# A hybrid decoder layer on one core: a third Strassen block in ten gate/up pairs, and the fold moved

## The reference

```python
def swiglu(h, w_gate, w_up, w_down):
    return (jax.nn.silu(h @ w_gate) * (h @ w_up)) @ w_down
...
        h = rmsnorm(x, norm_ffn_g[l])
        x = x + swiglu(h, w_ffn_gate[l], w_ffn_up[l], w_ffn_down[l])
    return rmsnorm(x, norm_final_g)
```

## Time and profile before

| | |
|---|---|
| median of 3 runs | 1755.81 us (1754.05 to 1756.22) |
| the profiled execution's own time | 1754.56 us |
| its span, first to last instruction | 1752.2 us |
| busy share: TensorE matmul, weight load, VectorE, ScalarE | 99%, 82%, 73%, 56% |
| granted TensorE clock, mean | 0.999 of full speed (2.4 GHz) |

### The profile page before, as it was taken

The page is one execution under the profiler, slowest core; times in us unless marked ns, Lnnn a source line. Parts: engine busy times, 40 slices in busy tenths (PEclk is TensorE's granted clock), DMA queues, the critical chain, the costliest instruction groups (busy, mean ns, idle before and its releaser), DMA issues.

```text
span 1752.2 us, 20308 instructions
## 1 busy us (share of the span) xinstructions
PE 1740.3 (99%) x7926; PEld 1444.7 (82%) x7926; DVE 1283.2 (73%) x1399; ACT 972.8 (56%) x1209; POOL 28.4 (2%) x54
## 2 busy tenths in 40 slices
PE   9999999999999999999999999999999999999998
PEld 7888888888888888888888888888888888888886
DVE  7577677887575757655565578888888788888787
ACT  6767678554555555544455465555545545555554
POOL 1000000000000000000000000000000000000000
PEclk9999999999999999999999999999999999999999
DMA  8565665666565655556755455566666565666664
GB/s 284 173 200 167 204 193 162 199 204 204 163 209 168 216 168 189 172 186 209 249 184 189 138 177 181 192 194 194 196 209 207 184 209 192 192 192 194 215 202 158
DMA packets 176047, 338.22 MB, mean 193 GB/s; under 512 B 10704, under 2 KB 15312, under 8 KB 175696
## 3 DMA queue, kind: packets, MB, share of 16 engines
q1 hardware_dynamic: 173232, 327.72, 59.3%
q0 software_dynamic: 1296, 5.24, 0.9%
q10 hardware_dynamic: 1424, 3.97, 0.6%
HBM read 334.80 MB, written 2.10 MB: 192 GB/s over the span
## 4 chain that ended last, share of the span: by engine, by line
PE 97%; DVE 1%; ACT 0%; DMA 0%; issue 0%; ACTq 0%; DVEq 0%; POOLq 0%; POOL 0%
PE group L468 29%; PE group L470 29%; PE group L469 29%; PE side L468 2%; PE side L469 2%; PE side L470 2%; PE side L531 2%; DVE w_lo L1199 0%; DMA x_T_in<-in_x_T 0%; PE side L649 0%; PE side L633 0%; PE side L587 0%; PE side L586 0%; PE side L585 0%; DVE x_res L1551 0%
## 5 line engine op out<-in xcount | busy, mean ns | idle before, releaser
L817 ACT ACTIVATE w_hi<-w_raw 128x1024 fp32r<-128x1024 f32 x612 | 622.9, 1029 | 543.5 <-PE group L470 447.9
L1199 DVE TENSOR_TENSOR w_lo<-w_raw,w_hi 128x1024 fp32r<-128x1024 f32 x612 | 712.6, 1186 | 286.3 <-ACT w_hi L817 280.3
L468 PE MATMUL group<-w_hi,x_hi 128*128 128x512 f32 x1466 | 575.6, 393 | 0.5 <-DVE w_lo L1274 0.3
L470 PE MATMUL group<-w_hi,x_lo 128*128 128x512 f32 x1466 | 571.0, 390 | 0.0
L469 PE MATMUL group<-w_lo,x_hi 128*128 128x512 f32 x1466 | 570.5, 389 | 0.0
L468 PEld LDWEIGHTS group<-w_hi,x_hi 128*128 128x128 f32 x1466 | 275.3, 188 | 58.9 <-DVE w_lo L1199 2.0
L470 PEld LDWEIGHTS group<-w_hi,x_lo 128*128 128x128 f32 x1466 | 275.1, 188 | 57.9
L469 PEld LDWEIGHTS group<-w_lo,x_hi 128*128 128x128 f32 x1466 | 275.4, 188 | 55.6
L817 ACT ACTIVATE w_hi<-w_sums 128x1024 fp32r<-128x1024 f32 x84 | 89.1, 1061 | 148.1 <-PE group L470 107.2
L1199 DVE TENSOR_TENSOR w_lo<-w_sums,w_hi 128x1024 fp32r<-128x1024 f32 x84 | 102.5, 1223 | 56.5 <-ACT w_hi L817 56.4
L468 PE MATMUL group<-w_hi,v_hi 128*128 128x512 f32 x296 | 115.9, 392 | 0.0
(11 more groups left out here) (304 smaller groups left out, 1707.4 us busy)
## 6 DMA issues: line engine op xcount, KB each, us to landing
w_raw<-in_w_in SPq DMA_DIRECT2D x223, 512.0 KB, 4.2
w_raw<-in_w_ffn_gate SPq DMA_DIRECT2D x88, 512.0 KB, 4.0
w_raw<-in_w_ffn_up SPq DMA_DIRECT2D x88, 512.0 KB, 4.6
w_raw<-in_w_ffn_down SPq DMA_DIRECT2D x88, 512.0 KB, 4.8
w_raw<-in_w_rnn_proj SPq DMA_DIRECT2D x32, 512.0 KB, 4.6
w_raw<-in_w_attn_proj SPq DMA_DIRECT2D x32, 512.0 KB, 4.3
w_raw<-in_w_mix_out SPq DMA_DIRECT2D x32, 512.0 KB, 4.6
w_raw<-in_w_xkv SPq DMA_DIRECT2D x16, 512.0 KB, 3.8
```

What stands on the lines that cost most here:

```text
L468: nc.tensor.matmul(out, h, whi[:, s, k, :], start=start, stop=False)
L470: return nc.tensor.matmul(out, l, whi[:, s, k, :], start=False, stop=stop)
L817: nc.scalar.activation(whi[:, s, ks], src[:, ks], ACT.Copy).then_inc(hi_ready[s], 1)
L1199: V_.tensor_tensor(wlo[:, s, ks], src[:, ks], whi[:, s, ks].bitcast(F32), ALU.subtract).then_inc(w_ready[s], 1)
```

## The change

The plan of the ten up pairs goes from two blocks to three: "O0 O1 W3 O2 O4 W5 O6 O7" becomes "O0 O2 W1 O4 W3 O6 W5 O7", 22 chunks instead of 20. The first up pair keeps a plan of its own with one block (W3). The sums of the left factor, made in that first pair, cover three blocks instead of two (k-pairs 1, 3, 5), in buffers of their own. In all pairs with blocks, ScalarE copies P1 in iteration last_sum-1 instead of last_sum+1. In the ten up pairs alone, where the last D stands third from the end, VectorE makes the first two additions of the fold in iteration last_sum and the other two in last_sum+1, one iteration sooner each than by the rule that holds elsewhere.

```diff
--- before.py
+++ after.py
@@ -62,7 +62,7 @@
 GROUPS += [("cross_out", _j, NB) for _j in range(KG)]
 
 
-UP_PLAN = "O0 O1 W3 O2 O4 W5 O6 O7".split()
+UP_PLAN = "O0 O2 W1 O4 W3 O6 W5 O7".split()
 RNN_PLANS = {0: "T0+1 O3 W2 O5 W4 O6 O7".split(), 2: "O0 O1 W2 O3 O5 W4 O6 O7".split()}
 KEY_PLAN = "O0 O1 W3 O2 O4 W5 O6 O7".split()
 FIRST_UP_PLAN = "O0 O1 O2 O4 W3 O5 O6 O7".split()
@@ -216,14 +216,18 @@
         chi = at("cross_hi", S + 8 * K1, [NB, SEQ], F32R)
         clo = at("cross_lo", S + 12 * K1, [NB, SEQ], F32R)
         fold = at("fold", S, [2, TT, GW])
-        both = at("x2_both", S + 4 * K1, [2, CK, SEQ])
-        x_sum = at("x2_sums", S, [2, 4, P])
-        xs_hi = at("x2_sums_hi", S + 12 * K1, [2, 4, P], F32R)
+        both = at("acts_both", S + 4 * K1, [2, CK, SEQ])
+        x_sum = at("acts_sums", S, [2, 4, P])
+        xs_hi = at("rnn_sums_hi", S + 12 * K1, [2, 4, P], F32R)
+        us_hi = at("x2_sums_hi", S + 8 * K1, [3, 4, P], F32R)
+        us = at("x2_sums", U + 24 * K1, [3, 4, P])
+        x2_both = at("x2_both", S, [3, CK, SEQ])
         fs_hi, fs_lo = at("inner_sums_hi", U + 24 * K1, [4, 4, P], F32R), at("inner_sums_lo", V + 24 * K1, [4, 4, P], F32R)
 
         STAGE = [region(4 * K1), region(4 * K1)]
         ks_hi = at("x_sums_hi", STAGE[0], [2, 4, P], F32R)
-        xs_lo = at("x2_sums_lo", STAGE[1], [2, 4, P], F32R)
+        us_lo = [at("x2_sums_lo0", STAGE[1], [2, 4, P], F32R), at("x2_sums_lo1", S + 14 * K1, [1, 4, P], F32R)]
+        xs_lo = at("acts_sums_lo", STAGE[1], [2, 4, P], F32R)
         stage = [at(f"stage{n}", STAGE[n], [TT, GW]) for n in range(2)]
         silu = stage[0]
 
@@ -515,13 +519,13 @@
                         products(P1, xh[:, k0, tok0], xl[:, k0, tok0], s, 0, begin, end)
                         last = products(gps[p0][:, 0, :], xh[:, k1, tok0], xl[:, k1, tok0], s, 1, False, False)
                     if kind == "B":
-                        last = products(gps[p1][:, 0, :], sh[:, w, 3, :], sl[:, w, 3, :], s, 1, False, False)
+                        last = products(gps[p1][:, 0, :], sh[:, w, 3, :], sl[w][:, 3, :], s, 1, False, False)
                     if kind == "C":
-                        products(Q5, sh[:, w, 0, :], sl[:, w, 0, :], s, 0, begin, end)
+                        products(Q5, sh[:, w, 0, :], sl[w][:, 0, :], s, 0, begin, end)
                         last = products(gps[p0][:, 1, :], xh[:, k1, tok1], xl[:, k1, tok1], s, 1, False, False)
                     if kind == "D":
-                        products(P7, sh[:, w, 2, :], sl[:, w, 2, :], s, 0, begin, end)
-                        last = products(P6, sh[:, w, 1, :], sl[:, w, 1, :], s, 1, begin, end)
+                        products(P7, sh[:, w, 2, :], sl[w][:, 2, :], s, 0, begin, end)
+                        last = products(P6, sh[:, w, 1, :], sl[w][:, 1, :], s, 1, begin, end)
                     last.then_inc(w_used[s], 1)
 
             def transpose(src, dst, done):
...
@@ -747,7 +751,7 @@
             for part, groups in (("a", FA), ("b", FB)):
                 for j in range(groups):
                     first = ("gate_" + part, j)
-                    for c, kind, kp in pair_of(first, xhi, xlo, xs_hi, xs_lo, X_SUMS):
+                    for c, kind, kp in pair_of(first, xhi, xlo, us_hi, (us_lo[0][:, 0], us_lo[0][:, 1], us_lo[1][:, 0]), X_SUMS):
                         if c == 2 and (part, j) == ("a", 0):
                             res_T("x2", GI["cross_out", KG - 1], KG - 1)
                         if c == 3 and j > 0:
...
@@ -779,7 +783,7 @@
             first = ("down_b", KG // 2)
             steps = STEPS[first]
             held = len(steps) - R
-            for c, kind, kp in pair_of(first, inner_hi, inner_lo, fs_hi, fs_lo, F_SUMS["b"], held):
+            for c, kind, kp in pair_of(first, inner_hi, inner_lo, fs_hi, [fs_lo[:, w] for w in range(4)], F_SUMS["b"], held):
                 if kind == "A" and kp == FIRST_SUM[first]:
                     pe.wait_ge(sem("folded"), folds)
 
@@ -850,8 +854,8 @@
 
             def first_fold(first, c):
 
-                if last_sum(first) is not None and c == last_sum(first) + 1:
-                    wait_product(act, N0[first] + c)
+                if last_sum(first) is not None and c == last_sum(first) - 1:
+                    wait_product(act, N0[first] + c - 1)
                     nc.scalar.activation(fold_of(first)[:, 0, 0, :], P1, ACT.Copy).then_inc(sem("fold_copied"), 1)
 
             squared = [0]
@@ -1137,7 +1141,7 @@
                                 gained_hi(side[1], 3, xhi, KG - 1, "x2_T", KG, "x2_hi")
                                 squares(xres, "x2", KG - 1)
                             if c == 1:
-                                sums_hi(xs_hi[:, :, :, :], x_sum[:, :, :, :])
+                                sums_hi(us_hi[:, :, :, :], us[:, :, :, :])
                         if j > 0:
                             if c == 0:
                                 gate_tanh(("gate_" + part, j - 1))
@@ -1348,13 +1352,14 @@
             def fold_rest(first, c):
 
                 at_, fold = last_sum(first), fold_of(first)
-                if at_ is not None and c == at_ + 1:
+                early = 1 if first[0].startswith(("gate", "up")) and at_ == len(STEPS[first]) - 3 else 0
+                if at_ is not None and c == at_ + 1 - early:
                     made[3] += 1
                     dve.wait_ge(sem("fold_copied"), made[3])
-                    wait_product(dve, N0[first] + c)
+                    wait_product(dve, N0[first] + at_ + 1)
                     then(V_.tensor_tensor(fold[:, 1, 0, :], fold[:, 0, 0, :], P6, ALU.subtract))
                     then(V_.tensor_tensor(fold[:, 0, 1, :], fold[:, 1, 0, :], P7, ALU.subtract))
-                if at_ is not None and c == at_ + 2:
+                if at_ is not None and c == at_ + 2 - early:
                     V_.tensor_tensor(fold[:, 1, 1, :], Q5, fold[:, 0, 1, :], ALU.subtract)
                     then(V_.tensor_tensor(fold[:, 1, 0, :], Q5, fold[:, 1, 0, :], ALU.subtract))
                     dve.sem_inc(sem("folded"), 1)
@@ -1642,11 +1647,13 @@
                                 halve("x2")
                             if c == 0:
                                 dve.wait_ge(sem("x2_lo"), KG - 1)
-                                picked = [x[:, :, :].rearrange("p (j b) t -> p j b t", b=NB)[:, 1:3, 2:4, :].bitcast(F32) for x in (xhi, xlo)]
-                                then(V_.tensor_tensor(both[:, :, :, :], picked[0], picked[1], ALU.add))
-                                sums_of(x_sum, both)
+                                picked = [x[:, :, :].rearrange("p (j b) t -> p j b t", b=NB)[:, 0:3, 2:4, :].bitcast(F32) for x in (xhi, xlo)]
+                                then(V_.tensor_tensor(x2_both[:, :, :, :], picked[0], picked[1], ALU.add))
+                                sums_of(us, x2_both)
                             if c == 2:
-                                sums_lo(xs_lo[:, :, :, :], x_sum[:, :, :, :], xs_hi[:, :, :, :])
+                                dve.wait_ge(sem("sums_hi"), made[2] + 1)
+                                V_.tensor_tensor(us_lo[1][:, 0], us[:, 2], us_hi[:, 2].bitcast(F32), ALU.subtract)
+                                sums_lo(us_lo[0][:, :, :, :], us[:, 0:2], us_hi[:, 0:2])
                         if j > 0:
                             if c == 0:
                                 gate_silu()
```

More of the change, by code:

```diff
@@ L594, in _ @@
                 first = ("rnn_out", q)
-                for c, kind, kp in pair_of(first, vhi, vlo, xs_hi, xs_lo, R_SUMS):
+                for c, kind, kp in pair_of(first, vhi, vlo, xs_hi, (xs_lo[:, 0], xs_lo[:, 1]), R_SUMS):
                     if q == 0 and c == 0:
@@ L610, in _ @@
                     first = ("k", j)
-                    for c, kind, kp in pair_of(first, xhi, xlo, ks_hi, xs_lo, K_SUMS):
+                    for c, kind, kp in pair_of(first, xhi, xlo, ks_hi, (xs_lo[:, 0], xs_lo[:, 1]), K_SUMS):
                         if kind == "A" and kp == FIRST_SUM[first]:
@@ L767, in _ @@
                 for q in range(0, KG if part == "a" else KG // 2, 2):
-                    for c, kind, kp in pair_of(("down_" + part, q), inner_hi, inner_lo, fs_hi, fs_lo, F_SUMS[part]):
+                    for c, kind, kp in pair_of(("down_" + part, q), inner_hi, inner_lo, fs_hi, [fs_lo[:, w] for w in range(4)], F_SUMS[part]):
                         if c == 3 and q == 0:
```

## The result

| | median (lowest to highest, runs) | ratio to before, 95% interval |
|---|---|---|
| before, run beside it | 1755.76 us (1754.05 to 1756.22, 4) | |
| changed kernel | 1767.7 us (1766.76 to 1768.69, 4) | 1.0072 [1.006, 1.0084] |

The change makes the kernel 12 us slower. The forecast was 1756.9 and the range ended at 1761.5. The profiled execution took 1768.44, its span is 1766.2, 14.0 longer than the span of before.

A forecast was written before the change was run, and what follows sets the result against it. TensorE's matmuls, busy 99%, were taken as the bound, if low parts keep ahead. Six summed pairs at +0.64 and four plain at -0.68 gave +1.1 us: 1756.9 from the 1755.81 median, range 1752.3 to 1761.5.

The forecast's parts named there:

- The walk through a summed pair: Order of three engines through an up pair with inner sums: two TensorE waits, 43.94 us for 43.30.
- A plain pair was given -0.68: Up pairs without inner sums: fewer matmuls, A3 ready 0.7 early, 42.36+0.05 us, counted four times.
- A summed pair was given +0.64: Up pairs with inner sums: two waits for low parts make 43.94 us for 43.30, counted six times.
- chunk 8's stop: First wait in a summed pair: low part made at 17.10, wanted by TensorE at 16.53; 0.63 us.
- the forecast 0.54: Second wait in a summed pair: A3 wanted at 22.79, started at 23.33, behind the second block's sums.
- The fold one iteration sooner: Fold additions in the up pairs: moves no work out of VectorE's unbroken stretch before the silu, so given nothing.
- the 4.4 on VectorE: Added VectorE work per pair: a block costs 6.7 us where an ordinary k-pair's two splits cost 2.28.
- the first pair at 0 to 0.3: First up pair's longer sums: 1.6 us later but covered by 0.2; cost 0, at most 0.3 us.
- nothing for the copy of P1: ScalarE's copy two chunks sooner in pairs with blocks: cost 0; without cover up to 0.5 in ten pairs.
- All hidden: Up pairs: no TensorE stop but today's, so -6.8 us, 1749.0; chance 0.14.
- Only the second wait: Summed pairs: chunk 8 as today, A3 late 0.55; -2.7 us in all, 1753.1; chance 0.12.
- The loads come late: W5 weight loads and the next pair's first chunks in up pairs: landings of 5.2 give +5.5, 1761.3; chance 0.18.

The follow-up runs named there:

- joins ahead: Changed kernel with the first join directly behind the third fold addition and the second one split later, same operations: 1759.95 us, ratio 1.0029.
- the best kernel: Changed kernel with both joins moved sooner and the inner sums seven iterations later, in iterations 11 to 13: 1752.55 us, ratio 0.9986.

## Why the prediction was wrong

**The step that failed** is in "The walk through a summed pair", in its first paragraph: "VectorE never stops on this stretch. The next pair starts at X+5.45 (24 matmuls)." The same paragraph has the fold and the first `join` ending at X+3.95+1.30+1.14 = X+6.39, which is 0.94 behind that start. The walk asked of each chunk whether its low part was made, and never whether the PSUM group it writes to was free. `join` is what frees it. The profile of before had a row for it, the `join` at 1205.44 with 1.3 us in hand, and it was not read. With the 0.94, the 0.06 of handover and 0.18 of restart, the text's own numbers give 1.18 for each of ten pairs, 11.8 us more less what the later start hides. Measured are 1.44 a pair: in the trace the `join` ends at X+6.70 (X is 1161.42), 0.3 later than the sum.

**The terms of the sum.** A plain pair was given -0.68 and measured +0.74: 42.41 and the 1.43 of the stop are the 43.83, within 0.01. A summed pair was given +0.64 and measured +1.46: there is the 1.44, and chunk 8's stop is 0.17 instead of 0.63, since TensorE itself begins late while VectorE goes on. The silu stands 3.3 behind the pair's start for the same reason (1171.44 and 1168.18), not 4.4. At chunk 10 the 0.72 are the sum of the forecast 0.54 and 0.18; the rows divide it into a start 0.60 late and 0.12 in the step behind it. Moving the joins ahead brought both forecast stops back (0.75 and 0.71) and the plain pair of 42.4, so the walk was right on the low parts; a summed pair then took 44.2 for 43.94, and the 0.25 at the C chunk was not in it. Two readings were a little off. TensorE alone needs 183 x 0.227 + 0.87 = 42.41, not 42.36, which the text made up for with its 0.05 in the plain pair. And of the 0.24 of today's summed pair the rows put only 0.16 at chunk 8 (0.06, and 0.10 in the step behind it).

**"The fold one iteration sooner moves no work out of the unbroken stretch, so I give it nothing."** Its second half, 1.3 us in the walk, now stands directly ahead of the first `join`, where a split stood between them before, as the rows of the order showed. It could not have stayed where the old rule puts it, in the pair's last iteration: there it would come behind the first `join`, which overwrites what the third addition reads. Taking only 0.6 of it and one split out from ahead of the `join` (joins ahead) was enough to end the wait. What moves nothing on its own engine still decides who behind it is served late.

**What was right:** the 30 matmuls and 0.227 a step, the 4.4 on VectorE, nearly (3.9 by the windows of a summed pair, 41.66 for 37.74), the first pair at 0 to 0.3 (0.09 and 0.06), nothing for the copy of P1 (0.9999), and no up pair in which L1218 waited for a load. "VectorE busy 97%" was 93%. The stops at chunks 8 and 10 were named as the only ones; the third, the longest, was not.

**The rivals.** *All hidden* fell: even with the joins ahead and the inner sums moved, summed pairs take 43.0 and not 42.4. *Only the second wait* was right for chunks 8 and 10 of the changed kernel (0.17 and 0.72), but by luck: chunk 8 is in time only because the `join` holds TensorE back, and with the joins ahead it costs 0.75. It was wrong for the time, as it lacked the `join` like the forecast. *The loads come late* was not seen in the up pairs; it was seen in a down pair, in the kernel with three blocks in the plain pairs alone. The time did fall on the slow side, by a mechanism that was in none of the rivals. The advice of the page on occupancy (the Trainium skill, Perfetto Trace Analysis, "Identifying the Most-Contended Engine") would have kept the forecast at 1749; the runs show VectorE busy only 93% of a pair, and TensorE waiting for it in every pair all the same.

**The semaphore's price.** The three weight sums of a block take 2.70 again (1187.12 to 1189.82 in the timeline of after). The rule that a semaphore adds nothing (the Trainium skill, VectorE: DVE Perf Modes, "The DRAIN you can't avoid"), by which they would be 2.36, is not what this trace shows for these sums; the page measured it on copies.

## What to carry to other kernels

A matmul of such a kernel waits for two things: its operands and the PSUM it writes to. In a walk over the order of the engines, each accumulator's release (here `join`) needs its own line with a due time, like each operand, and its slack today should be read from the trace before anything is put ahead of it. When a plan brings the costly work nearer to the end of a group, look at what frees that group, and put it ahead of the work that nobody waits for. What one stage gives can be lost in the next one that waits for loads, so the last mark of every stage is to be compared, not the first alone.

## What was not expected of the hardware

The granted clock had a mean of 0.79 between 12 and 20 us behind an idle of TensorE of 1.8 to 2.1, and stayed at 1.00 behind ones of 0.20, 0.26 and 0.62. The first transposes came 1.4 to 1.9 us later with it, in every profile with ten three-block pairs and four matmuls ahead of the first chunk. Why those programs step 0.23 in the first chunk and the others 0.43, with the same operations there, stays open. The kernel with three blocks in only four pairs stepped 0.23 too, idled 2.20, kept its clock, and came to the transposes at 57.07, so a long idle alone does not decide it. Nor is it settled that the program does: each profile is one execution, and single executions of one kernel differ. Of the ten of the best kernel four have a mean clock of 0.999 and took 1751.08 to 1752.47, six have 0.998 and took 1752.5 to 1754.21; with one matmul ahead eight of ten have 0.999. The kernel before has both values as well. Also open are 0.7 to 1.3 us that three kernels (joins ahead, the joins one iteration later, and the best one) lose between 296 and 424 us, where no edit touches anything; the changed kernel loses nothing there. Differences of about 2 us between these kernels are therefore not put down to an edit where no stop in the profile carries them.

A stop of TensorE costs more than its wait. At 1123.42 the wait shown is 1.15 and 1.43 are lost by the starts, at 1146.33 it is 0.44 and 0.72: 0.28 beside the idle time that the profile shows. The prediction's 0.18 is another measure: it counts from the moment at which the matmul was due, and so counted both stops have 0.12 beside the wait.
